# A four-tap depthwise convolution moved from VectorE to TensorE, with a gather ring of 13 rows in place of 19

## What is computed

```python
for l in range(DEPTH):                                   # 2
    n = rms_norm(h, attn_norm[l]); proj = n @ w_in[l]    # 1024 -> 3592
    y_gdn = gdn_mixer(gq, gk, gv, gz, gb, ga, gdn_conv[l], ...)
    ...
def gdn_mixer(...):
    qkv = silu(causal_depthwise_conv(concat([q, k, v]), conv_w))   # 4 taps, 1536 channels
    q, k, v = split(qkv); q = l2_norm(q); k = l2_norm(k)
    ...                                                  # gates, then the gated delta rule
def peer_ffn(x, w_q, sub_keys, u_tab, v_tab):
    ...                                                  # expert_idx: 8 heads x 16 for a token
    hid  = gelu(einsum('td,thkd->thk', x, u_tab[idx]))   # 128 rows of U for a token
    coef = gates * hid
    return einsum('thk,thkd->td', coef, v_tab[idx])      # 128 rows of V for a token
```

## Time and profile before

| | |
|---|---|
| time, median of 3 runs | 3575.7 us (3572.45 to 3588.38) |
| the profiled execution's own time | 3579.97 us |
| its span, first to last instruction | 3577.9 us |
| busy: PE, DVE, POOL, ACT | 2093.8, 2226.3, 2012.5, 822.8 us |
| instructions | 29,527 |
| HBM traffic in DMA packets | 1272.29 MB, 356 GB/s over the span |
| granted TensorE clock, mean | 0.752 of full |

### The profile page before, as it was taken

One profiled execution on the slowest core, in us unless ns is written; L12 is line 12 of the kernel. 1 busy time (PEld: TensorE's weight loads), 2 busy tenths in 40 slices (PEclk: granted clock), 3 DMA queues, 4 the chain that ended last, 5 costly groups with the idle time before them and its releaser, 6 DMA issues.

```text
span 3577.9 us, 29527 instructions
## 1 busy us (share of the span) xinstructions
PE 2093.8 (59%) x9038; PEld 1003.4 (28%) x9038; DVE 2226.3 (62%) x4995; ACT 822.8 (23%) x2485; POOL 2012.5 (56%) x2084
## 2 busy tenths in 40 slices
PE   7792565776744466595664357687573446632335
PEld 4541422343312332243221233234331232200001
DVE  4359866676577676756577666856558666664530
ACT  3212222232123131222223032213314112210211
POOL 1014565655567555656557655656546656666665
PEclk9796678897866668797777668789686767866558
DMA  8278899999999889999999989999898989999998
GB/s 295 78 260 314 292 386 409 404 409 341 390 392 354 318 337 409 382 383 354 348 409 387 373 306 408 381 376 407 330 393 327 341 322 373 406 376 368 384 363 338
DMA packets 349947, 1272.29 MB, mean 356 GB/s; under 512 B 37490, under 2 KB 37560, under 8 KB 348512
## 3 DMA queue, kind: packets, MB, share of 16 engines
q0 software_dynamic: 295744, 1075.38, 78.5%
q1 hardware_dynamic: 52752, 185.95, 13.7%
q10 hardware_dynamic: 1296, 9.08, 0.6%
HBM read 1264.07 MB, written 6.20 MB: 355 GB/s over the span
## 4 chain that ended last, share of the span: by engine, by line
PE 26%; DVE 18%; issue 16%; another core or an unknown queue 15%; POOL 13%; DMA 5%; ACT 5%; PEldq 0%; PEld 0%; SPq 0%; DVEq 0%; POOLq 0%; ACTq 0%
PE work L824 14%; POOL ring L438 13%; DVE ring L1122 6%; PE work L794 4%; PE accs L808 4%; DMA wring<-in_peer_wq 2%; PE work L785 2%; DMA ring<-in_peer_v,idxR 2%; DMA ring<-in_peer_u,idxU 1%; ACT arena L471 1%; DVE proj L1134 1%; DVE projB L1134 1%; DVE proj L1130 1%; ACT wv L499 1%
## 5 line engine op out<-in xcount | busy, mean ns | idle before, releaser
L438 POOL DMA_INDIRECT ring<-in_peer_u,idxU x1024 | 998.6, 975 | 847.2 <-issue 281.4
L438 POOL DMA_INDIRECT ring<-in_peer_v,idxR x1024 | 997.8, 974 | 673.6 <-issue 275.7
L1122 DVE CUSTOM_DVE_ANT_0 ring<-ring,n2U 128x1024 f32<-128x1024 f32 x1024 | 1199.6, 1218 | 267.2 <-DMA ring<-in_peer_u,idxU 212.8
L808 PE MATMUL accs<-ring,wv 128*32 128x512 f32 x4096 | 719.4, 800 | 637.9 <-DMA ring<-in_peer_v,idxR 362.8
L824 PE MATMUL work<-wring,nT 128*128 128x512 f32 (+1 forms) x1408 | 658.0, 616 | 97.2 <-DMA wring<-in_peer_wq 47.9
L808 PEld LDWEIGHTS accs<-ring,wv 128*32 128x32 f32 x4096 | 152.8, 133 | 1117.7 <-issue 1049.6
L824 PEld LDWEIGHTS work<-wring,nT 128*128 128x128 f32 x1408 | 283.5, 206 | 444.7 <-issue 363.4
L499 ACT ACTIVATE wv<-stack,coefR 128x32 f32<-128x32 f32 x1024 | 236.6, 309 | 400.8 <-remote 317.1
L471 ACT ACTIVATE arena<-work 128x512 f32<-128x512 f32 (+3 forms) x208 | 112.6, 563 | 612.0 <-remote 329.1
L794 PE MATMUL work<-arena 128*128 128x128 f32 x768 | 129.5, 331 | 143.2 <-issue 138.6
L824 PE MATMUL work<-wring,n2A 128*128 128x449 f32 x384 | 168.2, 559 | 10.2 <-issue 10.2
(11 more groups left out here) (290 smaller groups left out, 2057.1 us busy)
## 6 DMA issues: line engine op xcount, KB each, us to landing
wring<-in_w_in SPq DMA_DIRECT2D x80, 898.0 KB
wring<-in_peer_wq SPq DMA_DIRECT2D x64, 1024.0 KB
wring<-in_w_out SPq DMA_DIRECT2D x32, 1024.0 KB
ring<-in_peer_u,idxU POOLq DMA_INDIRECT x1024
ring<-in_peer_v,idxR POOLq DMA_INDIRECT x1024
arena<-keys_scr ACTq DMA_DIRECT2D x8, 1024.0 KB
keys_scr<-ring SPq DMA_DIRECT2D x2, 1024.0 KB, 4.9
hbuf<-in_x SPq DMA_DIRECT2D x1, 1536.0 KB, 15.8
```

Source lines behind the costliest of these rows:

```text
L438: nc.gpsimd.indirect_dma_start(ring[:, s * D:(s + 1) * D], None, table, bass.IndirectOffsetOnAxis(ap=idx, axis=0)).then_inc(row_in[s], 16)
L808: ins = nc.tensor.matmul(acc[c][quarter(r), :], wv[:, d * QUARTER:(d + 1) * QUARTER], ring[:, s * D + 512 * c:s * D + 512 * c + 512], star ...
L1122: V.tensor_tensor_reduce(out=rw, in0=rw, in1=n2U[:], scale=1.0, scalar=0.0, op0=ALU.mult, op1=ALU.add, accum_out=hid[:, kk:kk + 1]).then_i ...
```

## The change

The products and sums of the taps leave DVE. For each layer, DVE builds 48 diagonal matrices once (`diag`, 12 blocks x 4 taps, 128 x 128 each: three instructions over 128 x 2048, in step 0 for the first layer and in step 4 for the second). For each tile, PE multiplies `conv_x` of a block, shifted by the tap, with the diagonal of block and tap, and accumulates the four taps in PSUM: 48 products of 128 x 128 x 128. The shifted tokens are the stationary side, so that the result has tokens on partitions: the 12 transposes back and their three copies go, and ACT's SiLU reads PSUM and writes `proj`.

`diag` takes 24 KB of each partition, and `SLOTS` goes from 19 to 13, which is six slots of 4 KB. `PLAN` stays.

The order moves too. On PE the first two thirds of the convolution, the cumulated gates and the last third stand right behind place pj5, in a front step ahead of the last product of the projection. On DVE and ACT the normalisation of q and k comes right behind the gates; the rows of pj6, pj7, conv and cN, and in front steps the short convolution, come after it. In the other steps the short convolution comes before.

```diff
-SLOTS = 19
+SLOTS = 13
...
-    out += banks_of("pj", 2, front) + banks_of("pj", 3, front)
-    out += [f"{n}.{t}" for n in
-            ["sT0", "sT1", "gcum", "grow"]
-            + ["cN0", "cN1", "cN2", "qhT", "khT", "kbT", "kk", "qk", "qgT", "X0"]
+    short = [f"sT{i}.{t}" for i in range(2)]
+    out += banks_of("pj", 2, front) + ([] if front else short)
+    out += [f"{n}.{t}" for n in ("cN0", "cN1", "gcum", "grow", "cN2")]
+    out += banks_of("pj", 3, front) + (short if front else [])
...
-                act.wait_ge(S["conv_done"], nth("conv_done", k))
-                nc.scalar.activation(conv_y, conv_y, ACT.Silu).then_inc(S["silu_done"], 1)
+                for i in range(3):
+                    w = filled(f"cN{i}.{k}")
+                    nc.scalar.activation(proj[:, 512 * i:512 * i + 512], w[:], ACT.Silu).then_inc(free[BANK[f"cN{i}.{k}"][0]], 1)
...
-                for i in range(3):
-                    got(f"cN{i}.{k}", proj[:, 512 * i:512 * i + 512])
+                root(8)
+                proj_out(3)
...
+                def convolved(i):
+                    x3, w = v3(conv_x, 12, 131), fill(f"cN{i}.{k}")
+                    out_of(f"xT{i}.{k}")
+                    for b in range(4):
+                        for tap in range(TAPS):
+                            ins = nc.tensor.matmul(w[:, b * P:(b + 1) * P], x3[:, 4 * i + b, tap:tap + P], cut(diag, P, (4 * i + b) * TAPS + tap),
+                                                   start=(tap == 0), stop=(tap == TAPS - 1))
+                    filled(f"cN{i}.{k}", ins)
...
+                    if b == 5:
+                        if not front:
+                            short()
+                        pe.wait_ge(S["head_ready"], nth("head_ready", k))
+                        pe.wait_ge(S["diag_ready"], 3 * (1 + layer(k)))
+                        convolved(0)
+                        convolved(1)
+                        pe.wait_ge(S["g_ready"], nth("g_ready", k))
...
+                        heads(f"grow.{k}", [(gbc[:, h * P:(h + 1) * P], triu[:]) for h in range(GH)])
+                        convolved(2)
...
-                pe.wait_ge(S["silu_done"], nth("silu_done", k))
-                for i in range(3):
-                    flip(f"cN{i}.{k}", blocks(conv_y[:, 512 * i:512 * i + 512], 4))
...
+            def tap_diagonals():
+                for i in range(3):
+                    V.tensor_tensor(v3(cut(diag, 16 * P, i), 16, P), rep(ident[:], 1, 16), rep(par[:, P_CW + 16 * i:P_CW + 16 * i + 16], 2, P),
+                                    ALU.mult).then_inc(S["diag_ready"], 1)
...
-                def tap(t):
-                    link(V.tensor_tensor(t3, x3[:, :, t:t + P], rep(cw[:, :, t], 2, P), ALU.mult))
-                    link(V.tensor_tensor(y3, y3, t3, ALU.add), "conv_done" if t == TAPS - 1 else "dve_chain")
-                link(V.tensor_tensor(y3, x3[:, :, 0:P], rep(cw[:, :, 0], 2, P), ALU.mult))
-                tap(1)
...
                 link(V.tensor_tensor(v3(vb, 4, P), v3(vb, 4, P), rep(beta, 2, P), ALU.mult))
+                mix("pj6")
+                mix("pj7")
+                if front:
+                    short_conv()
+                mix("conv")
+                mix("cN")
                 mix("kbT")
```

More of the change, by code:

```diff
@@ L539, in stage_a, with short_in @@
                 mix("xT")
+                def short_in():
+                    got(f"sT0.{k}", sT[:, 0:512])
+                    empty(f"sT1.{k}", sT[:, 512:768], 256)
                 proj_out(2)
+                if not front_of(t):
+                    short_in()
                 act.wait_ge(S["gate_arg"], nth("gate_arg", k))
@@ L1171, in stage_a @@
                     emptied(f"xT{i}.{k}")
[L1172 to L1178 removed]
+                link(V.memset(hist, 0.0) if last else V.tensor_copy(v3(hist, 12, 3), x3[:, :, P:P + 3]))
                 mix("xT")
@@ L1185, in stage_a @@
                 link(V.tensor_tensor(ga1, ga1, xa, ALU.min), "gate_arg")
-                tap(2)
                 mix("pj5")
@@ L1189, in stage_a, with short_conv @@
                 link(V.tensor_scalar(ga1, ga1, 1.0, None, ALU.add), "gate_arg")
-                tap(3)
-                mix("pj6")
+                def short_conv():
+                    emptied(f"sT0.{k}")
+                    emptied(f"sT1.{k}")
+                    s3, sw = v3(xs, 2, P + 2), v3(par[:, P_SW:P_SW + 6], 2, SC_TAPS)
+                    ya_at = nT[:, 512:768]
+                    ya, yb = v3(ya_at, 2, P), v3(n2A[:, 768:1024], 2, P)
+                    link(V.tensor_copy(s3[:, :, 0:2], v3(shist, 2, 2)))
+                    link(V.tensor_tensor(s3[:, :, 2:P + 2], v3(sT[:, 256:512], 2, P), v3(sT[:, 512:768], 2, P), ALU.mult))
+                    link(V.tensor_tensor(ya, s3[:, :, 0:P], rep(sw[:, :, 0], 2, P), ALU.mult))
+                    for i in range(1, SC_TAPS):
+                        link(V.tensor_tensor(yb, s3[:, :, i:i + P], rep(sw[:, :, i], 2, P), ALU.mult))
+                        link(V.tensor_tensor(ya, ya, yb, ALU.add))
+                    link(V.tensor_tensor(ya_at, ya_at, sT[:, 0:256], ALU.mult), "ysc_ready")
+                    link(V.memset(shist, 0.0) if last else V.tensor_copy(v3(shist, 2, 2), s3[:, :, P:P + 2]))
                 dve.wait_ge(S["gate_ln"], nth("gate_ln", k))
```

72 lines of the change are left out of this document (31 added, 41 removed).

## The result

The changed kernel took 3722.49 us (median of 4 runs, 3717.78 to 3734.01), the kernel before 3574.07 us on the same chip (4 runs, 3570.42 to 3588.38): a ratio of 1.0393, with a 95% interval from 1.0364 to 1.0423. It is 3.9% slower, as forecast. The experiments show that the forecast arrived there by luck, by two errors that cancel, so the reasons are worth more than the number.

The account below looks back on a forecast made before the run. Bound by each tile's chain through DVE, PE and ACT, with row work woven in, and a supply whose best rate is a tenth above the draw. 3580 + 133 (ring) + 5 (direct) = 3718, said as 3715 us; range 3585 to 3840.

Parts of the forecast that it names:

- The ring: Row gathers: 13 slots in place of 19 leave less stock, so rows come late; 133 us, ends 0 and 248.
- The walk: All 2,048 gathers followed in order of PLAN with 13 slots: late rows end it 248 us later if nothing is absorbed.
- The rest stands inside the chain: Late rows in places with no wait of DVE behind them: all 98 us kept in the 133.
- The rival in which nothing is absorbed: Whole kernel: pauses pass from step to step, the full 248 us and the 5; 3830 us, chance 0.12.
- The direct part: Work moved between DVE, PE and ACT, without the thinner ring: +5 us, ends -45 and +45.
- Front steps: Steps 0, 2, 4, 6: convolution delays PE's last product 13.7 us, 9.5 us go behind it; +21 us in all.
- Odd steps: Steps 1, 3, 5, 7, first tap to transposes of q and k: a gain of 4 us each, -16 us.
- POOL's waits for PE and DVE: Sign of being right: POOL's idle time ended by PE and DVE rises well over 604 us.
- 96 MATMULs a tile: Sign in the convolution on PE: 96 MATMULs a tile, 14 us in front steps, up to 25 in the others.
- If below 3650, the ring term is the one: Sign on the total: a time below 3650 us would put the error in the ring term, the least known.
- the transfers bind anyway: Rival: DMA engines are at their limit, so the time stays at 3576 us; chance 0.11.
- DVE's time was the price: Rival: odd steps gain the full 12.3 us each and the thinner stock costs nothing; 3548 us, chance 0.09.

Follow-up runs that it names:

- new_ring19: The changed kernel with 19 slots and the identity in place of the diagonals, so the taps' values are left out: 3685.55 us, 1.0297 of the kernel before.
- new_order_alone: The changed kernel's order with 19 slots, but DVE's taps, one SiLU and twelve transposes where its products stand: 3673.55 us, 1.0228 of the kernel before.
- old_conv_alone: The kernel before, own order and 19 slots, convolution as 48 PE products with the identity, no DVE taps: 3308.97 us, 1.0018 of the kernel before.
- old_ring13: The kernel before with the ring cut from 19 to 13 slots and nothing else: 3628.55 us, 1.0141 of the kernel before.

## Why the prediction was right, and where its steps were wrong

**The total** came out: 3715 us forecast, 3722 us measured. That was luck: 86 us too much for the ring and 99 us too little for the rest. The mechanism that it named first, that rows come late when POOL is held, is in the trace.

**The ring, 133 us: mis-sized**, 47 us measured, 44 in the new order. The walk was right that rows come late; the step that failed is "The rest stands inside the chain", of which I kept all 98, and with it the 27 us of the selections and of nm to sc. Where I kept 83 us, 22 were gained. I had tested only three places for a wait behind a late row, and took the absence of a test for the absence of a wait. The better estimate was the other end: each engine of this kernel is idle for over a third of the span, so a late row often falls into someone's wait. The rival in which nothing is absorbed (248 us) missed by more still. By the ratios, 16 slots cost 28 us and 13 cost 50, so the price per slot is no steeper from 16 to 13 than from 19 to 16.

**The direct part, +5 us: wrong**, 104 us measured (90 to 123 by the interval). Its two steps:

- *Front steps.* "PE is later by 13.7 us and some wait, and 9.5 us are returned behind the product." In new_ring19 the last product of steps 2, 4 and 6 ends 36, 22 and 24 us later after the step's start than before (129, 137, 144 to 166, 160, 168), against 22, 15 and 15 expected; in the kernel after, 51, 14 and 23. From the product's end to `lt` it is 33.8, 25.4, 22.2 us before and 10.5, 34.8, 24.6 in new_ring19: 23 returned in step 2, and 9 and 2 lost in the others. I had counted what is removed from PE's list behind the product and not what is added to DVE's: the short convolution and all the dots behind it. For PE alone the 9.5 us came out, as step 4 of new_ring19 shows above. (The sum also has a slip: by its own figures step 2 is 13.7 + 8 - 9.5 = 12 us, not 9.)
- *Odd steps.* "A gain of 4 us a step", counting eight late dots as 9.8 us of DVE. PE's share was right: the convolution with the gates in it runs from 2003.09 to 2025.0 in step 5 (the 32 MATMULs of its last third end there), 22 us, inside the 16 to 28 us that the forecast had for them. In profiled runs steps 1, 3, 5 and 7 of new_ring19 are 4, 30, 5 and 15 us longer than before, not 4 shorter. Their 24 late dots, 29 us, make about half of these 54 us. The gain that was to outweigh them did not come: the taps leave DVE, but it then waits for `gcum`, which PE makes behind the first 32 products. DVE waits for ACT's copy of it for 90.5 us in the eight steps of new_ring19 and for 42.2 us in new_order_alone, which has no products there. (The 4 us had no working either: at the slow clock the sum of 35 us leaves 1 us of 36.)

**The signs.** POOL's waits for PE and DVE rose from 604 to 816 us: right, but the order alone would have given it too (750 us). DVE's waits for U rows grew from 212.8 to 484.7 us: right. That the odd steps would lose more to the ring than they gain was beside the point, since they gain nothing. Rate 341 GB/s: right, though it follows from the time alone. 96 MATMULs a tile: right (768). "If below 3650, the ring term is the one": a total could not test it. Only the two sizes run apart did.

**The rivals.** That the transfers bind anyway is ruled out by 1.0393. The Trainium skill's rule in "DMA: Bandwidth & Descriptors", section "Where 436 GB/s comes from", that the HBM side binds at about 358 GB/s for a core, is contradicted once more: old_conv_alone moves 1272.36 MB at 385 GB/s over its whole span. That DVE's time was the price: order and ring would have had to be free; old_conv_alone shows that even then 98 us of taps less on DVE, with the products added on PE, bring no gain (6 us slower). What the taps alone are worth was not run.

**Open.** On the slower chips the 82 us of the order are not split into late dots and PE's part; the 62 us are from the faster chips. The idle time that "remote" ends between scaled and `lt` (54 us in new_ring19, 2 us before) is part of the price there, and its cause is not known. A kernel that beats both was not found: old_conv_alone is 6 us behind the kernel before, and with real diagonals it would lose six slots, an estimated 47 us more.

## What to carry to other kernels

When work that filled an engine's wait is moved behind that wait, expect it to cost about its own length, here 63 us of dots and a kernel 62 us longer. If it is also the consumer of a ring, look at who is held while it is late, and whether the stock in the ring covers that pause: in steps 4 and 5 on the slower chips 19 slots mostly did and 13 did not. Work taken off an engine ahead of a wait brings only what the wait does not take back. And when a change has two parts, run the two parts apart before trusting an estimate of the whole, even one that came true.

## What the runs showed that I had not expected

**The same kernel on two kinds of chip.** The kernel before takes 3574 to 3586 us in the first three comparisons and 3303 us in the last two, 8% apart, each on a chip of its own. The waits of ACT tell them apart: first the kernel before on the chip of the first section, then old_conv_alone on a faster one.

```profile
ACT arena L471 <- remote: 329.1, 35, 25.9
ACT wv L499 <- remote: 317.1, 35, 23.6
```

```profile
ACT proj L471 <- PE work L823: 401.5, 46, 28.3
ACT wv L499 <- PE accs L807: 381.4, 77, 24.4
```

"Remote" is the profile's word for another core or an unknown queue. In the kernel before such waits of ACT add up to 929 us; in old_conv_alone there is none, and PE's idle time put down to issue is 85 us, against 533. In new_ring19 they are 1055 us. One in new_ring19, step 6, in ACT's copies of the eight normalised transposes, all finished by PE at 2390.94, in the middle of an unbroken burst of gathers:

```profile
2391.76 1.14 ACT L484 ACTIVATE nT<-work,par 128x128 f32<-128x128 f32 x4 [2.80 <-issue]
2400.18 1.14 ACT L484 ACTIVATE n2A<-work,par 128x128 f32<-128x128 f32 x4 [7.27 <-remote]
2410.68 1.14 ACT L484 ACTIVATE n2A<-work,par 128x128 f32<-128x128 f32 x4 [9.36 <-remote]
```

The first product of that step waits 21 us for them. In old_ring13 these waits sum to 724 us, so a thinner ring may have given some of its cost back that way; this was not tested, and what the releaser is, and whether anything else ran on the slower chips, stays open.

**On the faster chips the rate is 409 GB/s in most slices** (old_conv_alone):

```profile
GB/s 302 63 218 403 286 391 409 408 409 386 409 409 409 409 390 410 409 408 400 410 409 409 409 394 409 409 408 388 397 410 409 408 409 410 409 404 398 403 409 370
```

Late dots cost 62 us there all the same. It may be that a pause of POOL is not made up later when the supply runs at its best rate; no run tests this, and the dots' own length accounts for the price without it.
